# The second block's feed-forwards: seven block products a tile pair instead of eight, in a three-pass fp32r kernel

## The reference, cut to what matters

```python
def rmsnorm(x, g):
    y = xf * lax.rsqrt(jnp.mean(xf * xf, axis=-1, keepdims=True) + EPS_2)
    return (y * g).astype(x.dtype)

def swiglu_2(x, w_gate, w_up, w_down):          # (1024 x 2816), (1024 x 2816), (2816 x 1024)
    return (jax.nn.silu(x @ w_gate) * (x @ w_up)) @ w_down

h = h + 0.5 * swiglu_2(rmsnorm(h, ffn1_norm[i]), ffn1_w_gate[i], ffn1_w_up[i], ffn1_w_down[i])
```

## Time and profile before

| what | value |
|---|---|
| runs of the kernel | 3566.03, 3568.04, 3570.75 us; median 3568.04 |
| profiled execution, its own time | 3568.63 us |
| its span, first to last instruction | 3566.8 us |
| granted TensorE clock, mean | 0.995 |
| busy: TensorE, weight load, VectorE, ScalarE, POOL | 98%, 78%, 44%, 36%, 12% |
| HBM read | 288.22 MB |

### The profile page before, as it was taken

How to read it: one execution, slowest core, us unless ns; L and a number is a source line. 1 busy time by engine, 2 the same in 40 slices (tenths; PEclk the granted TensorE clock), 3 DMA queues, 4 the chain that set the end, 5 groups by cost and what they waited for, 6 DMA issues and landing times. The chain is left out here.

```text
span 3566.8 us, 41802 instructions
## 1 busy us (share of the span) xinstructions
PE 3486.0 (98%) x15766; PEld 2771.5 (78%) x15790; DVE 1572.8 (44%) x2139; ACT 1285.3 (36%) x1802; POOL 443.5 (12%) x366
## 2 busy tenths in 40 slices
PE   9999999999999999999999999999999999999998
PEld 7788788867778886888876688877888886688885
DVE  3387433356643334333366733335333256733325
ACT  4353422245432224332343533235332333533324
POOL 0001111000201101221000022102221000022102
PEclk9999999999999999999999999999999999999999
DMA  4201233222122322333220233313333220132322
GB/s 147 88 1 47 78 95 110 95 72 66 42 83 94 105 95 65 95 102 106 78 70 16 71 100 94 114 59 99 95 99 109 75 84 19 53 100 94 112 71 77
DMA packets 78030, 292.06 MB, mean 82 GB/s; under 512 B 8657, under 2 KB 11473, under 8 KB 77649
## 3 DMA queue, kind: packets, MB, share of 16 engines
q1 hardware_dynamic: 77328, 289.31, 25.4%
q10 hardware_dynamic: 576, 1.05, 0.1%
HBM read 288.22 MB, written 2.10 MB: 81 GB/s over the span
## 5 line engine op out<-in xcount | busy, mean ns | idle before, releaser
L157 DVE TENSOR_TENSOR w_low<-w_raw,w_high 128x1024 fp32r<-128x1024 f32 (+4 forms) x513 | 672.6, 1311 | 1521.0 <-ACT w_high L152 1520.9
L191 PE MATMUL bank<-x_high,w_high 128*128 128x512 f32 x2856 | 1118.9, 392 | 20.7 <-DVE w_low L157 9.2
L193 PE MATMUL bank<-x_high,w_low 128*128 128x512 f32 x2856 | 1111.6, 389 | 0.0
L192 PE MATMUL bank<-x_low,w_high 128*128 128x512 f32 x2856 | 1111.4, 389 | 0.0
L152 ACT CAST w_high<-w_raw 128x1024 fp32r<-128x1024 f32 (+4 forms) x513 | 555.0, 1082 | 846.6 <-PE bank L193 838.1
L191 PEld LDWEIGHTS bank<-x_high,w_high 128*128 128x128 f32 x2856 | 536.2, 188 | 147.5 <-DVE w_low L157 14.4
L193 PEld LDWEIGHTS bank<-x_high,w_low 128*128 128x128 f32 x2856 | 536.2, 188 | 112.0
L192 PEld LDWEIGHTS bank<-x_low,w_high 128*128 128x128 f32 x2856 | 536.3, 188 | 111.4 <-issue 1.7
L191 PE MATMUL bank<-hidden_high,w_high 128*128 128x512 f32 x1056 | 410.8, 389 | 0.0
L192 PE MATMUL bank<-hidden_low,w_high 128*128 128x512 f32 x1056 | 410.8, 389 | 0.0
L193 PE MATMUL bank<-hidden_high,w_low 128*128 128x512 f32 x1056 | 410.8, 389 | 0.0
(11 more groups left out here) (543 smaller groups left out, 3446.8 us busy)
## 6 DMA issues: line engine op xcount, KB each, us to landing
w_raw<-in_stream SPq DMA_DIRECT2D x381, 512.0 KB, 3.5
w_raw<-in_stream SPq DMA_DIRECT2D x96, 704.0 KB, 4.0
w_raw<-in_stream SPq DMA_DIRECT2D x16, 384.0 KB, 3.1
w_raw<-in_stream SPq DMA_DIRECT2D x4, 576.0 KB, 3.7
dft_positions<-in_dft SPq DMA_DIRECT2D x2, 1024.0 KB, 4.8
w_raw<-in_stream SPq DMA_DIRECT2D x16, 128.0 KB, 2.1
out<-result SPq DMA_DIRECT2D x4, 512.0 KB, 2.7
h<-in_x ACTq DMA_DIRECT2D x4, 256.0 KB, 6.2
```

What stands on the lines that cost most here:

```text
L157: self.nc.vector.tensor_tensor(self.lo[:, j % 2, 0:size], self.raw[:, j % RAW_SLOTS, 0:size], self.hi[:, j % 2, 0:size].bitcast(F32), ALU. ...
L191: nc.tensor.matmul(out, lhs[0], rhs[0], start=start, stop=False)
L192: nc.tensor.matmul(out, lhs[0], rhs[1], start=False, stop=False)
L193: return nc.tensor.matmul(out, lhs[1], rhs[0], start=False, stop=stop)
```

## The change

The up part of a feed-forward becomes, for each pair of a gate tile and an up tile, one 2 x 2 block product by seven products instead of eight. The blocks of the weights are (gate, up) x (features 0 to 511, features 512 to 1023): a11 and a12 are the halves of the gate job, a21 and a22 of the up job. The blocks of the input are (features 0 to 511, 512 to 1023) x (tokens 0 to 255, 256 to 511): x11, x12, x21, x22. VectorE forms four sums of weight blocks for each pair (`sum_one` to `sum_four`, in the raw slots and `s_one`) and, once a stage, four sums T1 to T4 of input blocks. Each of the seven weight operands ("units" 0 to 6; the first split makes units 0 and 1 together, a 1024-column piece, the others are 512 columns) is split by ScalarE and VectorE into a place of its own in `units_high` and `units_low`, which is free when the same product of the pair before is done. A product is 4 feature tiles x 3 passes, 12 matmuls of 256 columns. Three banks serve a pair: bank a gathers products 0, 2, 4 and 6, bank b products 3 and 5, bank e product 1; between these ScalarE copies the partial sums out (`copy_out` of products 0, 2, 3 and 4, into p1, u2, p5, u3), and VectorE adds them to the gate's and the up tile's halves.

The sums of input blocks need the input with 1/rms in it, so VectorE writes `x_work` = h x gain x rstd at the entry, 8 tiles, and x11, x21 and x22 are split from it into the places of `x_high` and `x_low` when the first three pairs (`CLASSIC`), which run as before, are through with them. `rstd` no longer follows behind silu in the other 19 pairs. `rstd_chain` moves to the front of ScalarE's list, `row_sums` of layer 1's ffn1 ahead of job 0.

The hidden tiles are kept in chunks of 6, 6, 5 and 5 (`CHUNKS`), and the down product is run chunk by chunk: after a chunk's pairs, 8 down jobs of 6 or 5 tiles each, and each adds to `h`: 32 residuals instead of 8. The weight stream is packed in this order (`strassen_jobs`). The last tile of a chunk is not ready at once, so down job 0 runs up to its last tile, then 3 tiles of job 1, then the rest of both. The first pair of the next chunk has its sums and units made at down step 6 (VectorE) and 5 (ScalarE). The low half of the hidden tile (`hidden_low`) moves from POOL to VectorE. All loops of the stage are written out, SP's as well, where a raw slot is fetched again when unit 5 (gate) or 6 (up) of its pair is split. The output is computed as before otherwise.

```diff
...
+HALF = T // 2
+CHUNKS = (6, 6, 5, 5)
+CLASSIC = 3
...
+                def product(f, kind, bank, high, low, start):
+                    pe.wait_ge(S.unit_low, units(f, kind))
+                    for q in range(HALF_T):
+                        at = slice((kind * HALF_T + q) * P, (kind * HALF_T + q + 1) * P)
+                        first, last = start and q == 0, q == HALF_T - 1
+                        nc.tensor.matmul(bank, uhi[:, at], high[:, q, :], start=first, stop=False,
+                                         skip_group_check=True)
+                        nc.tensor.matmul(bank, uhi[:, at], low[:, q, :], start=False, stop=False,
+                                         skip_group_check=True)
+                        mm = nc.tensor.matmul(bank, ulo[:, at], high[:, q, :], start=False, stop=last,
+                                              skip_group_check=True)
+                    mm.then_inc(S.used, 1)
+
+                def pair(f):
+                    g = strassen(f)
+                    a, b, e = (C.bank[3 * (f % 2) + i][:, left] for i in range(3))
+                    pe.wait_ge(S.hid_ready, f - 1)
+                    if g == 0:
+                        pe.wait_ge(S.gate_in, CLASSIC)
+                        pe.wait_ge(S.t_low, T1 + 1)
+                        product(f, 3, b, thi[:, T1, :, :], tlo[:, T1, :, :], True)
+                        pe.wait_ge(S.b_low, B11 + 1)
+                    product(f, 0, a, operands[B11][0], operands[B11][1], True)
+                    if g == 0:
+                        pe.wait_ge(S.b_low, B21 + 1)
+                        pe.wait_ge(S.hid_ready, CLASSIC)
+                    product(f, 1, e, operands[B21][0], operands[B21][1], True)
+                    pe.wait_ge(S.copied, 4 * g + 1)
+                    if g == 0:
+                        pe.wait_ge(S.t_low, T2 + 1)
+                    product(f, 2, a, thi[:, T2, :, :], tlo[:, T2, :, :], False)
+                    if g:
+                        product(f, 3, b, thi[:, T1, :, :], tlo[:, T1, :, :], True)
+                    pe.wait_ge(S.copied, 4 * g + 2)
+                    product(f, 4, a, thi[:, T3, :, :], tlo[:, T3, :, :], False)
+                    pe.wait_ge(S.copied, 4 * g + 3)
+                    if g == 0:
+                        pe.wait_ge(S.b_low, B22 + 1)
+                    product(f, 5, b, operands[B22][0], operands[B22][1], False)
+                    pe.wait_ge(S.copied, 4 * g + 4)
+                    if g == 0:
+                        pe.wait_ge(S.t_low, T4 + 1)
+                    product(f, 6, a, thi[:, T4, :, :], tlo[:, T4, :, :], False)
+
+                def down(c, d, tiles):
+                    n, j = CHUNKS[c], down_job(c, d)
+                    if tiles[0] == 0:
+                        pe.wait_ge(S.low_ready, 2 * CLASSIC + DT * c + d + 1)
+                        if DT * c + d >= 2:
+                            pe.wait_ge(S.residual_done, DT * c + d - 1)
+                    for q in tiles:
...
+                for c, n in enumerate(CHUNKS):
+                    for f in range(max(CLASSIC, first_pair(c)), first_pair(c + 1)):
+                        pair(f)
+                    down(c, 0, range(0, n - 1))
+                    down(c, 1, range(0, 3))
+                    down(c, 0, range(n - 1, n))
+                    down(c, 1, range(3, n))
+                    for d in range(2, DT):
+                        down(c, d, range(n))
...
+                for c, n in enumerate(CHUNKS):
+                    for f in range(max(CLASSIC, first_pair(c)), first_pair(c + 1)):
+                        last = f == first_pair(c + 1) - 1
+                        ahead = f > first_pair(c) and f > CLASSIC
+                        g, i, j = strassen(f), 2 * CLASSIC + DT * c, down_job(c, 0)
+                        a, b = C.bank[3 * (f % 2)], C.bank[3 * (f % 2) + 1]
+                        if g:
+                            act.wait_ge(S.added, 3 * g - 2)
+                        copy_out(f, 0, a, p1)
+                        if ahead:
+                            silu(f - 1)
+                        unit(f, 6)
+                        if last:
+                            high(i, j)
+                        else:
+                            unit(f + 1, 0)
+                        if g:
+                            act.wait_ge(S.added, 3 * g)
+                        copy_out(f, 2, a, u2)
+                        copy_out(f, 3, b, p5)
+                        if last:
+                            high(i + 1, j + 1)
+                        else:
+                            unit(f + 1, 2)
+                        if g:
+                            act.wait_ge(S.hid_ready, f)
+                        copy_out(f, 4, a, u3)
+                        if not last:
+                            unit(f + 1, 3)
+                        if ahead:
+                            hidden_high(f - 1)
+                        if not last:
+                            unit(f + 1, 4)
+                            unit(f + 1, 5)
...
+                dve.wait_ge(S.rstd_in, 1)
+                for t in range(DT):
+                    if t == 5:
+                        gate_classic(0)
+                        low(2, 2)
+                    nc.vector.scalar_tensor_tensor(work[:, t, :], C.h[:, t, :], norm(t), C.rstd[:, :], ALU.mult,
+                                                   ALU.mult).then_inc(S.x_made, 1)
+                dve.wait_ge(S.x_made, DT)
+                sums_made(T1, x12, x11, 0)
+                low(3, 3)
+                sums_made(T3, x22, x12, 0)
+                hidden_classic(0)
+                sums_made(T2, x22, sums[:, T1, :, :], 1)
+                gate_classic(1)
+                hidden_low(0)
+                low(4, 4)
+                sums_made(T4, x21, sums[:, T2, :, :], 3)
+                sums_low(T1)
+                sums_low(T3)
+                hidden_classic(1)
+                low(5, 5)
+                sums_low(T2)
+                f = CLASSIC
+                sum_one(f)
+                sums_low(T4)
+                sum_three(f)
+                unit(f, 0)
+                gate_classic(2)
+                hidden_low(1)
+                sum_two(f)
+                sum_four(f)
+                for kind in range(2, 5):
+                    unit(f, kind)
+                unit(f, 5)
+                hidden_classic(2)
+                operand_low(B11)
+                operand_low(B21)
+                operand_low(B22)
+                hidden_low(2)
...
+                        last = f == first_pair(c + 1) - 1
+                        ahead = f > first_pair(c) and f > CLASSIC
+                        i, j = 2 * CLASSIC + DT * c, down_job(c, 0)
+                        unit(f, 6)
+                        if not last:
+                            sum_one(f + 1)
+                        else:
+                            low(i, j)
+                        gate_left(f)
+                        if not last:
+                            sum_three(f + 1)
+                            unit(f + 1, 0)
+                        if ahead:
+                            hidden_left(f - 1)
+                        if not last:
+                            sum_two(f + 1)
+                        if ahead:
+                            hidden_right(f - 1)
+                        if not last:
+                            sum_four(f + 1)
+                            unit(f + 1, 2)
+                        else:
+                            low(i + 1, j + 1)
+                        up_right(f)
+                        if not last:
+                            unit(f + 1, 3)
+                        if ahead:
+                            hidden_low(f - 1)
+                        if not last:
+                            unit(f + 1, 4)
+                        gate_right(f)
+                        if not last:
+                            unit(f + 1, 5)
+                    hidden_left(f)
+                    hidden_right(f)
+                    hidden_low(f)
+                    for d in range(DT):
+                        if d + 2 < DT:
+                            low(2 * CLASSIC + DT * c + d + 2, down_job(c, d + 2))
...
```

More of the change, by code:

```diff
@@ L944, in _ @@
[L944 to L956, removed]
@@ L985, in _ @@
[L985 to L992 removed]
+                rstd_chain(nc, C, act, S, C.bank[summed or 6])
@@ new lines, in _ @@
+                high(2, 2)
+                silu(0)
+                high(3, 3)
+                sums_high(T1)
+                sums_high(T3)
+                sums_high(T2)
+                high(4, 4)
+                hidden_high(0)
+                silu(1)
+                sums_high(T4)
+                high(5, 5)
+                f = CLASSIC
+                unit(f, 0)
+                hidden_high(1)
+                silu(2)
+                for kind in range(2, 6):
+                    unit(f, kind)
@@ new lines, in hidden_low, with gate_left @@
+                def hidden_low(f):
```

(36 more changed lines are left out.)

317 lines of the change are left out of this document (235 added, 82 removed).

## The result

The changed kernel takes 3580.7 us (median of 8 runs, 3578.5 to 3583.8) against 3568.9 (8 runs): a ratio of 1.0034, interval 1.0025 to 1.0043. It is slower, by 11.8 us, where 9 us less were forecast. Its profiled execution has a span of 3582.0 us, 15.2 more than that of before; 2.3 of these are there before 160 us, where nothing was changed.

A forecast was written before the change was run, and what follows sets the result against it. TensorE's matmul count and spacing were taken as the bound. Per stage -15.05 + 1.1 + 7.6 + 4.1 = -2.25 us, -9.0 over four stages, from 3568.0 to 3559.0 us; range for 8 in 10: 3540 to 3583.

The forecast's parts named there:

- what a pair costs TensorE: Products: 84 matmuls at 120.0 ns, 10.08 us instead of 10.87 a pair, saving 15.05 us a stage.
- rival (4): Products: 256-column steps slower than 120 ns; at 129.4 TensorE gains nothing and waits stay, 3610 us; chance 0.03.
- The seams: Start of a chunk's down work: job 2 waits for residual 0, 0.8 or 1.25 us each, 4.1 us a stage.
- The ring: Middle pairs: product 6 waits for ScalarE's copy of product 4, 0.10 us a pair, 1.1 us a stage.
- Rival (1): Middle pairs become a VectorE loop; break-even 0.30 us lost a pair, at 0.5 3577 us, slower; chance 0.18.
- Rival (3): Entry and pairs cost less than listed, as ScalarE and VectorE use each other's slack: 3535 to 3548 us; chance 0.14.
- the entry: Stage start: TensorE waits for VectorE's list up to the first input block and in the first pair, 7.6 us a stage.
- The 24 added residuals lie there too: Down work: the added residuals lie under down jobs 6 and 7 and cost nothing.
- the entry's term for POOL: Stage start: three POOL multiplications lengthen VectorE's work beside them, 0.6 us a stage in all.
- rival (2): Clock falls at the stage-start wait: 0.2 to 1.7 us a stage, 3560 to 3566; chance 0.25, including mixed small losses.
- The sign: Whole kernel: faster 0.53, same 0.26, slower 0.21; 9.0 us less forecast over four stages.
- The 4.9 us at which VectorE was to begin in ffn2: Stage start in ffn2: VectorE begins its list 4.9 us after job 0's start, once rstd is ready.

The follow-up runs named there:

- e8: The changed kernel plus one unused 512-column VectorE addition ahead of the first weight sum in the 11 middle pairs of each stage: 3601.5 us.
- e2: The changed kernel with VectorE writing the residual ahead of the low half in the last chunk's down jobs 1 to 7 only: 3563.9 us.
- e3: The changed kernel with weight job 4 cast ahead of T2's high half, its low half ahead of the first hidden tile's, at the entry: 3574.5 us.
- e7: e3 plus residuals ahead of low halves (job 6: behind next units), and sum_four, lows of T4, units 4, 5, hidden tile 1 moved behind x11: 3546.3 us.
- e9: e7 with the low halves of the input sums T3 and T2 also moved behind those of x11 and x21 on VectorE: 3551.2 us.
- e10: e7 with product 4's copy ahead of the next pair's unit 2 on ScalarE, hidden_right ahead of sum_two on VectorE, every pair: 3537.0 us.
- e13: e10 with the three entry multiplications by 1/rms moved from POOL to VectorE: 3532.5 us, ratio 0.9899.

## Why the prediction was wrong

**Right:** what a pair costs TensorE (120.0 ns a step, 15.05 us a stage), so rival (4) falls. The seams, to 0.1 us. The ring's place, with a term 0.18 too long a pair: unit 2 starts 0.03 behind sum_two's end (1523.95 to 1523.98) where 0.09 were put down, the rest is hundredths, and so 1.1 us became 0. e8 shows how little slack is left. Rival (1) did not occur, but an addition of 0.6 us a pair is enough to make it. Rival (3) did not occur either, since the entry cost more than listed.

**Failed, first:** the end of the stage. "The 24 added residuals lie there too" was meant of all chunks, and put nothing down for the last, where VectorE also makes the next stage's input and first weight tiles. There a residual behind a low half, with a round trip to ScalarE between two residuals, repeats every 3.98 us against TensorE's 3.40, 0.63 of them through POOL's addition beside the low half, and leaves the last two residuals late: 1.8 + 1.6 us a stage and 1.65 of half clock after the two longer hand-overs. e2 takes it away and gets 17 us.

**Failed, second:** the entry's term for POOL, 0.6 us a stage for three multiplications. It measured 3.1, 2.5 more. The entry came out 2.5 too short, in part by chance the same: 0.4 of that is the clock. The 1.43 us row was taken as the price of such a neighbour; but POOL's multiplication there ran from 1398.27 to 1399.57 and VectorE's row began at 1399.22: 0.21 us more for 0.35 shared. In all these rows, those of the last chunk too, VectorE's is longer by what POOL's instruction still had to run when it began, less 0.13 to 0.2: 0.35 gave 0.21, 0.44 gave 0.31, 0.77 gave 0.64, 1.12 gave 0.98, 1.23 gave 1.03 and 1.10. The Trainium skill ("SBUF — State Buffer", SBUF: two separate sides) says that VectorE, with two inputs in SBUF, and a GpSimd instruction that reads SBUF share a port pair that one holds for a whole instruction while the other is blocked. These rows agree.

**The clock,** rival (2): it falls at the entry, and costs 1.7 us in all there, almost all of it in the one stage where no wait for VectorE follows; the forecast had 0.2 to 1.7 in each stage. What half clock costs behind the hand-over was not tried alone.

**The sign** rests on the end of the stage: without it, and with the entry as it measured, the change comes to -15.05 + 10.1 + 4.0 = -0.95 us a stage, and e2 stands at 0.9988.

**In the sum itself** three numbers do not follow from what stands beside them. The 4.9 us at which VectorE was to begin in ffn2 is 5.44 less 0.87, 4.6, by the earlier trace rows; the trace has 5.0, so this came out by luck. The 256-column copy is 0.36 and not 0.39 by the prices given; it measured 0.37. Rival (4)'s 3610 is 3615 by its own entry and seams.

## What to carry to other kernels

Give the last pass of a loop its own line in the sum: what prepares the next stage runs there beside the work that repeats, and here one queue order set the hand-over. Price an instruction by what runs beside it: here POOL's neighbours put 3.1 us on the entry's list and 0.63 on each of four down jobs. On a path bound by one engine's list, moving items within it gave back no more than that engine's own idle time (e3), next to nothing (e7), or a loss (e9); the gain came from a short copy that no longer waits in another queue for the list (e10), and from taking the neighbour away (e13). Before a step is hidden under a ring, count the ring's slack: here 0.08 us of 10.08.

## What was not expected of the hardware

A POOL instruction of 512 columns, 1.3 to 1.6 us long, holds up the VectorE instruction that begins beside it for nearly as long as it still has to run: 0.21 to 1.1 us here, whether that is a subtraction of 640 or 1024 columns, a sum of 512 or scalings. An instruction of VectorE under which POOL's begins is not longer (1735.80, 0.75 us, with POOL's from 1736.37). Moving one of the entry's multiplications to VectorE costs 0.8 us and saves 1.0.
